# Modulation weights of the first block's feed forwards: two contraction tiles by 1024 columns in place of eight by 256

## What is computed

```
silu_c = jax.nn.silu(c)
silu_cc = jax.nn.silu(c_ctx)
for layer in range(DEPTH):
    mod_x = silu_c @ ada_w[layer] + ada_b[layer]
    mod_c = silu_cc @ ada_w[layer] + ada_b[layer]
    sh1, sc1, g1, sh2, sc2, g2 = [m[:, None, :] for m in jnp.split(mod_x, 6, axis=-1)]
```

```
def squared_relu_mlp(h, w1, w2):
    a = jax.nn.relu(h @ w1)
    return (a * a) @ w2
```

## Time and profile before

| | |
|---|---|
| median of three runs | 3636.82 us |
| span of the profiled execution, first to last instruction | 3635.2 us |
| TensorE (PE) busy | 3455.9 us, 95% of the span |
| weight loads (PEld) busy | 2750.8 us, 76% |
| VectorE (DVE) busy | 2014.6 us, 55% |
| ScalarE (ACT) busy | 1205.8 us, 33% |
| GpSimd (POOL) busy | 226.8 us, 6% |
| chain that ended last | TensorE 88%, VectorE 8%, ScalarE 3% |
| mean granted TensorE clock | 0.971 of full |
| HBM, mean over the span | 87 GB/s |

### The profile page before, as it was taken

How to read it: one execution, slowest core, us unless ns; L and a number is a source line. 1 busy time by engine, 2 the same in 40 slices (tenths; PEclk the granted TensorE clock), 3 DMA queues, 4 the chain that set the end, 5 groups by cost and what they waited for, 6 DMA issues and landing times.

```text
span 3635.2 us, 42169 instructions
## 1 busy us (share of the span) xinstructions
PE 3455.9 (95%) x17456; PEld 2750.8 (76%) x17456; DVE 2014.6 (55%) x3705; ACT 1205.8 (33%) x2017; POOL 226.8 (6%) x314
## 2 busy tenths in 40 slices
PE   7989999999989999998999889999998998799998
PEld 6647688887867688887986567888886885478886
DVE  5564587896664578884125675333335235664334
ACT  5353432225453332223112233332333212243332
POOL 0200000001040000000000001000001000000000
PEclk9999999999999999999999799999999999889999
DMA  5302144442212154443210021122122310113331
GB/s 169 103 18 92 63 157 152 162 139 87 75 29 81 53 168 162 154 147 128 80 62 28 9 80 47 59 60 68 59 66 80 112 59 30 41 58 95 98 97 58
DMA packets 210011, 317.00 MB, mean 87 GB/s; under 512 B 5304, under 2 KB 154426, under 8 KB 208540
## 3 DMA queue, kind: packets, MB, share of 16 engines
q1 hardware_dynamic: 194012, 243.00, 20.8%
q0 software_dynamic: 15808, 71.31, 5.8%
HBM read 300.66 MB, written 14.49 MB: 87 GB/s over the span
## 4 chain that ended last, share of the span: by engine, by line
PE 88%; DVE 8%; ACT 3%; issue 1%; DMA 0%; SPq 0%; DVEq 0%; ACTq 0%
PE ps L94 87%; DVE t L115 4%; ACT t L100 3%; DVE t L107 2%; PE ps L97 1%; DVE t L111 1%; DVE t L125 0%; DVE t L121 0%; DVE ps L115 0%; DVE t L118 0%; DVE ps L107 0%; DMA t<-in_mem 0%; DVE t L112 0%; ACT L100 0%; DMA t<-in_ctx 0%
## 5 line engine op out<-in xcount | busy, mean ns | idle before, releaser
L94 PE MATMUL ps<-t,t 128*128 128x512 f32 (+6 forms) x17040 | 3401.5, 364 | 148.1 <-DVE t L115 67.6
L94 PEld LDWEIGHTS ps<-t,t 128*128 128x128 f32 (+3 forms) x17040 | 2700.6, 189 | 822.8 <-issue 168.6
L100 ACT ACTIVATE t<-t 128x1024 fp32r<-128x1024 f32 (+5 forms) x1158 | 819.5, 742 | 1256.6 <-PE ps L94 924.3
L107 DVE TENSOR_TENSOR t<-t,t 128x1024 fp32r<-128x1024 f32 (+6 forms) x790 | 724.6, 947 | 581.0 <-ACT t L100 575.3
L100 ACT ACTIVATE t<-ps 128x512 f32<-128x512 f32 (+7 forms) x442 | 222.5, 529 | 805.9 <-PE ps L94 767.5
L115 DVE SCALAR_TENSOR_TENSOR t<-t,t,t 128x256 f32<-128x256 f32 (+3 forms) x927 | 437.7, 535 | 13.6 <-ACT t L100 7.3
L107 DVE TENSOR_TENSOR t<-ps,t 128x512 f32<-128x512 f32 (+4 forms) x293 | 188.8, 661 | 206.1 <-PE ps L94 144.0
L115 DVE SCALAR_TENSOR_TENSOR t<-ps,t,t 128x512 f32<-128x512 f32 (+1 forms) x252 | 154.6, 661 | 254.6 <-PE ps L94 234.4
L107 POOL TENSOR_TENSOR t<-t,t 128x64 f32<-128x64 f32 (+1 forms) x208 | 143.4, 713 | 1721.1 <-ACT t L100 1576.0
L118 DVE COPY t<-ps 128x256 f32<-128x256 f32 (+3 forms) x162 | 73.0, 479 | 278.3 <-PE ps L94 259.7
L100 ACT ACTIVATE t<-t,t 128x512 fp32r<-128x512 f32 (+3 forms) x160 | 96.0, 603 | 194.0 <-DVE t L107 127.9
(11 more groups left out here) (33 smaller groups left out, 295.9 us busy)
## 6 DMA issues: line engine op xcount, KB each, us to landing
t<-in_w_ff SPq DMA_DIRECT2D x64, 1024.0 KB, 5.3
t<-in_w_mlp SPq DMA_DIRECT2D x64, 1024.0 KB, 5.4
t<-in_ada_w POOLq DMA_DIRECT2D x48, 1024.0 KB, 5.8
t<-in_w_in SPq DMA_DIRECT2D x30, 1024.0 KB, 5.3
t<-in_w_qkv_o SPq DMA_DIRECT2D x12, 1024.0 KB, 5.1
t<-in_w_mem_kv SPq DMA_DIRECT2D x8, 1024.0 KB, 7.1
t<-in_w_mem_q SPq DMA_DIRECT2D x8, 1024.0 KB, 5.1
t<-in_w_mem_o SPq DMA_DIRECT2D x8, 1024.0 KB, 5.1
```

The costliest lines, as they stand in the source:

```text
L94: return Issued(self, self.e and self.e.matmul(o, l, r, start=start, stop=stop, skip_group_check=True))
L100: return Issued(self, self.e and self.e.activation(o, i, f, **kw))
L107: return Issued(self, self.e and self.e.tensor_tensor(o, a, b, op))
```

## The change

Load b of a layer now holds 2 of the 8 contraction tiles, number 2(b % 4) and the next, of 1024 output columns, from 1024(b // 4). Four loads in a row make one accumulation over all 8 tiles. A load is 1 MB as before, in pieces of 4 KB for each row of the weight where they were 1 KB, in the same buffers and at the same steps. VectorE does 4 operations of 128x1024 on it where it did 16 of 128x256. `ACC` is 1024 columns wide. TensorE sums the partitions only after each fourth load, 16 matmuls of 128x1 in a row where it did 4 after every load, and VectorE adds the bias for them in one operation of 128x16 from bank 7. Consumers wait for group 5 of `mod` where they waited for group 23.

```diff
-            f.ACC = [ar([128, 2, 256]) for _ in range(2)]
+            f.ACC = [ar([128, 2, 1024]) for _ in range(2)]
...
                 b = mod_steps.index(s - 1)
+                if b % 4 < 3:
+                    return
                 pe.wait_ge("macc", l, b, 1)
                 opening(7)
-                for m in range(2):
+                for m in range(8):
                     for c in range(2):
-                        ins = pe.matmul(P[7][:, 2 * m + c:2 * m + c + 1], tiles.ACC[b % 2][:, c, 128 * m:128 * m + 128],
+                        ins = pe.matmul(P[7][:, 2 * m + c:2 * m + c + 1], tiles.ACC[b // 4 % 2][:, c, 128 * m:128 * m + 128],
                                         cst("ones", 128, 1), True, True)
-                ins.then_inc("mps", l, b)
-                free[7] = [("mod", l, b)]
+                ins.then_inc("mps", l, b // 4)
+                free[7] = [("mod", l, b // 4)]
...
-                if l is not None and s - 1 in mod_steps:
-                    b = mod_steps.index(s - 1)
+                if l is not None and s - 1 in mod_steps and mod_steps.index(s - 1) % 4 == 3:
+                    b = mod_steps.index(s - 1) // 4
                     dve.wait_ge("mps", l, b)
-                    for m in range(2):
-                        k = 2 * b + m
-                        ins = dve.tensor_scalar(MOD[l][:, k, :], P[7][:, 2 * m:2 * m + 2], vec(f"ada_b{l}", k), None, ALU.add)
...
+                    bias = vec(f"ada_b{l}", 8 * b, 8).rearrange("p (k c) -> p k c", c=1).broadcast_to([128, 8, 2])
+                    dve.tensor_tensor(MOD[l][:, 8 * b:8 * b + 8, :], P[7][:, 0:16].rearrange("p (k c) -> p k c", c=2), bias,
+                                      ALU.add).then_inc("mod", l, b)
...
-                    wv = tiles.ADA[s % 2][:, :].rearrange("p (k n) -> p k n", k=8)
-                    acc = tiles.ACC[s % 2]
+                    wv = tiles.ADA[s % 2][:, :].rearrange("p (k n) -> p k n", k=2)
+                    acc = tiles.ACC[s // 4 % 2]
...
-                    for kk in range(8):
+                    for kk in range(2):
                         for c in range(2):
-                            x, o, w = SIL[:, kk, c:c + 1], acc[:, c, :], wv[:, kk, :]
-                            if kk == 0:
-                                dve.tensor_scalar(o, w, x, None, ALU.mult).then_inc("macc0", l, s, c)
+                            x, o, w = SIL[:, 2 * (s % 4) + kk, c:c + 1], acc[:, c, :], wv[:, kk, :]
+                            if kk == 1:
+                                dve.wait_ge("macc0", l, s, c)
+                            elif s % 4 > 0:
+                                dve.wait_ge("macc", l, s - 1, c)
+                            if s % 4 == 0 and kk == 0:
+                                ins = dve.tensor_scalar(o, w, x, None, ALU.mult)
                             else:
...
                                 ins = dve.scalar_tensor_tensor(o, w, x, o, ALU.mult, ALU.add)
...
+                            ins.then_inc("macc" if kk else "macc0", l, s, c)
...
-            dve.wait_ge("mod", l, 23)
+            dve.wait_ge("mod", l, 5)
...
-                dst = FF1.ADA[b % 2][:, :].rearrange("p (k n) -> p k n", k=8)
-                pl.dma_start(dst, rows(A["ada_w_2"][l])[:, :, 256 * b:256 * b + 256]).then_inc(s_ada[b % 2], "ada", l, b)
+                dst = FF1.ADA[b % 2][:, :].rearrange("p (k n) -> p k n", k=2)
+                k0, c0 = 2 * (b % 4), 1024 * (b // 4)
+                pl.dma_start(dst, rows(A["ada_w_2"][l])[:, k0:k0 + 2, c0:c0 + 1024]).then_inc(s_ada[b % 2], "ada", l, b)
```

More of the change, by code:

```diff
@@ L2011, in modulate @@
+                            if s % 4 == 0 and kk == 0:
+                                ins = dve.tensor_scalar(o, w, x, None, ALU.mult)
                             else:
-                                dve.wait_ge(*(("macc0", l, s, c) if kk == 1 else ("maccp", l, s, kk - 1, c)))
                                 ins = dve.scalar_tensor_tensor(o, w, x, o, ALU.mult, ALU.add)
[L2014 to L2017, removed]
+                            ins.then_inc("macc" if kk else "macc0", l, s, c)
```

## The result

The changed kernel takes 3657.6 us (median of four runs, 3657.2 to 3661.4) against 3638.1 (3636.8 to 3644.1) for the kernel before on the same chip: 1.0052 times as long, 95% interval 1.0037 to 1.0066. The forecast was slower, 3647.3, with a range up to 3656: the direction was right, and the 10.5 us forecast are half of what came. The profiled execution took 3657.59 us with a span of 3655.8, 20.6 us more than the span before; that pair is what the traces can explain.

The account below looks back on a forecast made before the run. TensorE was taken to bound the feed forwards, with VectorE hidden. Terms for VectorE, loads, TensorE's work and the wait were 0, the clock 10.5 us: 3645.7 against the span of 3635.2, 3647.3 us as median, range 3635 to 3656.

Parts of the forecast that it names:

- VectorE: hidden, worth 0: Feed forwards: wide accumulations at 1.19 us apiece relieve VectorE by about 42 us a layer, hidden behind TensorE, worth 0.
- Loads: 0: Weight loads in the feed forwards: same 1 MB at the same steps, landing well within a 12 us step, worth 0.
- TensorE's own work: 0, cost by record: Partition sums in the feed forwards: same 96 a layer, cost set by record and not by group, worth 0.
- Rival 2: Sums in the feed forwards: 36 fewer switches between large and small matmuls save TensorE time, 11 us, time 3626; chance 4%.
- The new wait: 0: VectorE's bias addition in a group's step may wait some 0.3 us for the last sum, covered by TensorE's matmuls; 0.
- TensorE's clock: Feed forwards: 3.6 us groups of sums move little data, so the clock halves behind seven of twelve; 10.5 us lost.
- rival 1: Groups of sums in the feed forwards are harmless, weight loads keep the clock up, all else hidden; 3636.8 us; chance 28%.
- The price of a fall: One stretch at half clock behind a group: 3.4 us long, 1.5 us lost; a 6.8 us one would lose 3.1.
- The rest of the kernel: Outside the feed forwards: the change touches nothing there, so no term was added to the sum.

## Why the prediction was right or wrong

**VectorE: hidden, worth 0.** Right. 1.19 us was taken for a wide accumulation, 1.22 measured; relief 42 us forecast, 42 and 46 measured (the 46 in a stretch in which the falls also let less of VectorE's work come by). The spread-out sums show that it is worth nothing that can be measured.

**Loads: 0.** Right; the same run has the same loads. They landed 5.6 us after issue where it was 5.8.

**TensorE's own work: 0, cost by record.** Right: 22.9 us for the sums in groups of 32 records, 22.7 in groups of eight, 11.0 when the records were halved. Rival 2, gain from fewer switches, is out.

**The new wait: 0.** Right for the change: TensorE never waited. Of the six bias additions of the first feed forward four did not wait at all; two waited 0.35 and 0.66 us (0.3 was forecast for each), behind the two groups that a fall had lengthened. In the run with the old accumulations TensorE did wait for VectorE, 1.5 and 1.1 us in the two stages.

**TensorE's clock.** The step that failed is the size of this term, 7 x 1.5 = 10.5 us: the falls in the two feed forwards cost 15.6 us. The mechanism and its place were right: falls right behind or in the groups and nowhere else in the stage, and rival 1 (weight loads keep the clock up) is refuted by the pair of 1 and 128 columns. That seven were forecast and seven came is luck: seven was a choice between 0 and 12, and the same grouping had six falls in the profile with 32 columns and eleven in the one with the old accumulations. TensorE was busy for 380.00 of 380.00 us in both stages, and the clock fell. The trace therefore agrees with the rule of the Trainium skill (TensorE: Matmul & The Clock Gate, "Why this matters for your kernels"), which speaks of idle gaps between bursts of matmuls, only if a gap is read as time in which little is moved; read as idle time it would have given no loss. Two things were mis-sized:
- *The price of a fall*, taken as 1.5 us with the 6.8 us kind left aside. Three of the seven lasted 6.8 us. The loss for each us at half clock was right: 13.6 us of falls cost 6.2 us in the second feed forward, 0.46 each, as 1 - 1/1.85 says. Four short ones at 1.56 and three long ones at 3.1 make 15.5 us, and the milestones show 9.4 + 6.2 = 15.6. The row that showed a 6.8 us stretch was dismissed because small matmuls ran in it; the long falls are those that began 0.7 to 1.5 us before the end of their group, with sums running in them at half pace. So the other ground for the low price, that sums under a fall are bound by their weight loads and lose nothing, was wrong too: the three groups took 3.8 to 4.2 us, where one takes 3.5 at full clock.
- *The rest of the kernel*, taken as unmoved. 4.5 us of falls in the attention came on top. They were read against a profile that had none; later runs of the unchanged kernel had a median up to 3642.7, and 3657.6 is 15 to 17.5 us above the three later medians, near the 15.6 us of the feed forwards alone. That this part is chance of the comparison and no cost of the change is likely, but not shown.

With 15.5 in place of 10.5 the same sum gives 3652, within the range; the 4.5 us in the attention carry the measured time past its end. That end, 3656, left out falls of the longer kind and anything outside the feed forwards, which made it too low.

## What to carry to other kernels

When TensorE is the bound, look at its granted clock, not at its busy share: a run of matmuls that load weights and move one column each is busy and can still bring the clock down, and then the dense work behind it pays. Gathering such small work into fewer, longer groups saved nothing here, since it costs by the record; keep it in pieces between dense matmuls, or make it shorter, or let it move more columns (128 cost no more than one here and kept the clock up, 32 did not keep it up). And compare with more than one profile before explaining a few us in a stage with loose matmuls.

## What the runs showed of the hardware

- One-column float32 matmuls in a row, one profile each: 1.7 us, no fall in 24 groups; 2.6 us, seven in twelve; 3.5 us, seven in twelve (eleven in the run with the old accumulations).
- A 128-column float32 record behind its own weight load costs no more than a one-column record: 22.4 / 192 = 0.117 us against 22.7 / 192 = 0.118.
- A float32 sum is two records, an fp32r sum one, at 0.11 to 0.12 us each either way.
- At half clock the sums go at about half pace too. The group that began at 643.9 us took 4.2 us where one at full clock takes 3.5; its fall began 1.5 us before its end, so sums worth 0.8 us took 1.5. The mean of a record was 329 ns under the fall from 513.5 us on, against 239 in the earlier trace rows:

```profile
L94 PE MATMUL ps<-t,t 128*128 128x1 f32 x5 | 1.1, 329 | 0.0
```
